# Storing new matrix-memory states from GpSimd's queue instead of SyncE's

## The reference

```
def mlstm_chunk_step(carry, inp):
    c_prev, n_prev, m_prev = carry
    q, k, v, ig, lf = inp
    ...
    num = jnp.einsum('bhls,bhsv->bhlv', s, v) + inter[..., None] * jnp.einsum('bhld,bhdv->bhlv', q, c_prev)
    ...
    c_new = decay[..., None, None] * c_prev + jnp.einsum('bhld,bhlv->bhdv', wk, v)
    n_new = decay[..., None] * n_prev + jnp.sum(wk, axis=2)
```

## Time and profile before

| what | value |
|---|---|
| three runs | 1604.52, 1608.56 and 1610.1 us; median 1608.56 |
| the profiled execution | 1613.31 us, of which the span from the first to the last instruction is 1611.6 |
| mean granted clock of TensorE | 0.914 of full speed |
| bytes moved | 532.80 MB, 331 GB/s over the span |
| stores of new states | 32 of 1024 KB |
| the matrix memory stage | about 130 to 306 us of the span |

### The profile page before, as it was taken

How to read it: one execution, slowest core, us unless ns; L and a number is a source line. 1 busy time by engine, 2 the same in 40 slices (tenths; PEclk the granted TensorE clock), 3 DMA queues, 4 the chain that set the end, 5 groups by cost and what they waited for, 6 DMA issues and landing times.

```text
span 1611.6 us, 18493 instructions
## 1 busy us (share of the span) xinstructions
PE 1336.9 (83%) x7591; PEld 748.0 (46%) x7593; DVE 519.6 (32%) x1217; ACT 191.6 (12%) x429; POOL 34.0 (2%) x72
## 2 busy tenths in 40 slices
PE   9999999999999766775785899999996656756866
PEld 6664332477754431332332577777543323323423
DVE  5647775532032220221121233630322212211222
ACT  2143232200020000000000211200200000000001
POOL 4001000000000000000000000000000000000000
PEclk8999998999989987888888999999999889888979
DMA  7335999976619999999999964452499999999995
GB/s 211 105 105 211 392 384 390 354 261 244 278 53 421 427 428 427 428 429 428 429 428 429 404 245 157 163 212 101 179 429 428 427 428 427 428 428 429 429 428 219
DMA packets 101532, 532.80 MB, mean 331 GB/s; under 512 B 6568, under 2 KB 24168, under 8 KB 76584
## 3 DMA queue, kind: packets, MB, share of 16 engines
q1 hardware_dynamic: 98536, 527.14, 80.8%
q10 hardware_dynamic: 2312, 4.20, 0.7%
q0 software_dynamic: 624, 0.62, 0.2%
HBM read 492.45 MB, written 39.49 MB: 330 GB/s over the span
## 4 chain that ended last, share of the span: by engine, by line
PE 56%; DMA 35%; DVE 4%; issue 2%; ACT 1%; SPq 1%; POOL 0%; DVEq 0%; ACTq 0%
DMA arena<-in_moe_w_up 28%; PE bank L922 24%; PE bank L1308 11%; PE bank L1330 5%; DMA out_C_s<-arena 4%; PE bank L1288 3%; PE bank L1343 3%; DMA arena<-in_state_mlstm_C 2%; PE bank L1316 1%; SPq L414 1%; PE bank L1213 1%; PE bank L1061 1%; ACT arena L786 1%; PE bank L1222 1%; PE bank L1396 1%
## 5 line engine op out<-in xcount | busy, mean ns | idle before, releaser
L1308 PE MATMUL bank<-arena,hT 128*32 128x512 f32 x2048 | 270.6, 688 | 191.4 <-DMA arena<-in_moe_w_up 178.4
L922 PE MATMUL bank<-hT,arena 128*128 128x288 f32 x1024 | 264.4, 417 | 3.3 <-issue 2.0
L1308 PEld LDWEIGHTS bank<-arena,hT 128*32 128x32 f32 x2048 | 75.0, 125 | 373.8 <-issue 373.4
L922 PEld LDWEIGHTS bank<-hT,arena 128*128 128x128 f32 x1024 | 195.7, 194 | 63.2 <-issue 5.6
L1850 DVE TENSOR_TENSOR arena<-arena,bank 64x512 f32<-64x512 f32 x32 | 22.1, 692 | 533.9 <-ACT arena L786 533.9
L1288 PE MATMUL bank<-arena 128*128 128x128 f32 (+1 forms) x864 | 157.8, 313 | 1.2 <-DVE arena L1825 0.9
L1330 PE MATMUL bank<-arena 128*32 128x512 f32 x1024 | 129.8, 651 | 21.2 <-DVE arena L1854 21.2
L1288 PEld LDWEIGHTS bank<-arena 128*128 128x128 f32 (+1 forms) x864 | 120.2, 192 | 49.6 <-issue 16.4
L922 PE MATMUL bank<-arena 128*128 128x288 f32 x512 | 127.9, 409 | 0.0
L922 PEld LDWEIGHTS bank<-arena 128*128 128x128 f32 x512 | 96.1, 190 | 30.8 <-issue 3.5
L786 ACT ACTIVATE arena<-bank 64x512 f32<-64x512 f32 x32 | 18.9, 589 | 759.6 <-PE bank L1308 759.6
(11 more groups left out here) (353 smaller groups left out, 980.6 us busy)
## 6 DMA issues: line engine op xcount, KB each, us to landing
arena<-in_moe_w_gate SPq DMA_DIRECT2D x64, 2048.0 KB, 28.4
arena<-in_moe_w_up SPq DMA_DIRECT2D x64, 2048.0 KB, 32.1
arena<-in_moe_w_down SPq DMA_DIRECT2D x64, 2048.0 KB, 25.2
arena<-in_state_mlstm_C SPq DMA_DIRECT2D x32, 1024.0 KB, 8.6
out_C_s<-arena SPq DMA_DIRECT2D x32, 1024.0 KB, 11.0
arena<-in_cmlp_w_in SPq DMA_DIRECT2D x8, 2048.0 KB, 17.5
arena<-in_mlstm_w_up SPq DMA_DIRECT2D x7, 2048.0 KB, 9.9
arena<-in_mlstm_w_down SPq DMA_DIRECT2D x4, 2048.0 KB, 18.1
```

The costliest lines, as they stand in the source:

```text
L922: ins = mm(B[m % 4][:, 0:NT], w[:, k, 128 * i:128 * i + 128], rhs(k), start=(k == 0), stop=(k == kt - 1))
L1308: ins = mm(B[j][CAP * i:CAP * i + CAP, :], xq[h][:, k, CAP * e:CAP * e + CAP], w[i][:, k, :], start=(k == 0), stop=(k == KD - 1), skip_gro ...
```

## The change

SyncE's loop keeps the waits for the stores, the loads of the states and the loads of the z pages; the waits for new states and the stores themselves go to GpSimd. There the loop over heads is written anew: the masks of head 0 come first; then, for each head, eight times a wait for a new state and its store, then the masks of the next head, then the store and the load of the normalisers as before. The semaphores are the same.

```
--- before.py
+++ after.py
@@ -361,18 +361,12 @@
             for q in range(6):
                 sp.wait_ge(s("xm_mm"), 4 * (q // 2 + 2))
                 load_state(q)
-            for q in range(NB * H + 1):
-                if q < NB * H:
-                    sp.wait_ge(s("c_new"), MH * (q + 1))
-                    sp.dma_start(state(O["C_s"], q), cview(q)).then_inc(s(f"c_stored{q % 2}"), 16)
-                if q > 0:
-
-                    r = q - 1
-                    sp.wait_ge(s(f"c_stored{r % 2}"), 16 * (r // 2 + 1))
-                    if r + 6 < NB * H:
-                        load_state(r + 6)
-                    elif r % 2 == 1:
-                        load_z((r - 27) // 2)
+            for r in range(NB * H):
+                sp.wait_ge(s(f"c_stored{r % 2}"), 16 * (r // 2 + 1))
+                if r + 6 < NB * H:
+                    load_state(r + 6)
+                elif r % 2 == 1:
+                    load_z((r - 27) // 2)
 
             sp.wait_ge(s("nums_mm"), H)
             sp.wait_ge(s("cv_stored"), 128)
@@ -515,7 +509,7 @@
                            allow_slow_non_contiguous=True).then_inc(s("m_stored"), 16)
             pool.dma_start(O["m_s"][0].rearrange("b h -> h b"), rows[32:36, NPROMPT + 3:NT:SB],
                            allow_slow_non_contiguous=True).then_inc(s("m_stored"), 16)
-            for h in range(H):
+            def masks_of_weights(h):
 
                 pool.wait_ge(s("e_ready"), 3 * (h + 1))
                 keep(ew[:, 0:128], [[1, P]], 0, -1).then_inc(s("e_masked"), 1)
@@ -523,6 +517,14 @@
                 es = ew[0:NS, 384:416].rearrange("p (b t) -> p b t", t=SB)
                 link(keep(es, [[SB, NB], [1, SB]], 0, -1))
                 keep(es, [[-SB, NB], [0, SB]], 0, 1).then_inc(s("e_masked"), 1)
+
+            masks_of_weights(0)
+            for h in range(H):
+                for q in range(NB * h, NB * h + NB):
+                    pool.wait_ge(s("c_new"), MH * (q + 1))
+                    pool.dma_start(state(O["C_s"], q), cview(q)).then_inc(s(f"c_stored{q % 2}"), 16)
+                if h + 1 < H:
+                    masks_of_weights(h + 1)
                 pool.wait_ge(s("ns_out"), h + 1)
                 pool.dma_start(n_out[h], nrow[:, h % 2, :]).then_inc(s(f"n_stored{h % 2}"), 16)
                 if h + 2 < H:
```

## The result

The changed kernel takes 1705.11 us (median of 4 runs, 1701.61 to 1707.15), the kernel before 1606.54 us beside it (4 runs, 1600.71 to 1610.1): a ratio of 1.0618, 95% interval 1.0587 to 1.0648. The forecast was 1605.3 us within 1597 to 1619. The time lies 86 us above the top of that range; the loss of 98.6 us has the sign that was given 0.25. One run further on is left out of median and ratio: experiment 1 had a tenth run of 1870.95 us at a mean granted clock of 0.674, where its nine others had 0.914 to 0.917.

A forecast was written before the change was run, and what follows sets the result against it. It took DMA transfers, almost saturated from 148 to 294 us, as the stage's bound. Start -0.3, saturated part -3.0, end 0 and GpSimd's queue 0 gave -3.3 us: 1608.6 to 1605.3 us, range 1597 to 1619.

The forecast's parts named there:

- the sign that was given 0.25: Whole kernel: the change makes it slower, chance 0.25, against 0.43 for the same and 0.32 for faster.
- the one on GpSimd's queue: Stores behind GpSimd's masks, small DMAs and `n_out` wait: delays to stores 8 and 16 covered by queued loads, 0 us.
- Rival C: GpSimd's stores cost more than SyncE's throughout: lower rate, slow issue or held issue; +6 to +10 us, chance 0.09.
- Masks: about as much time as before: 0: GpSimd's masks of the next head, now behind eight stores but ahead of the `n_out` wait: 0 us.
- rival D: VectorE's bursts of four updates hold up GpSimd's store issues, three times 2.7 us: +8 us, chance 0.03.
- Rival B: GpSimd gates the ends of heads 0 and 1, store 8 waiting until `n_out` lands: +6 us, chance 0.13.
- The gain at the start: From 142 to 148 us, loads 7 and 8 no longer stand behind stores of states not yet new: -1.7 us.
- The saturated part: From 148 to 294 us, half the distance from 392 to 409 GB/s is gained: -3.0 us (range 0 to -6.1).
- Rival A: SyncE's queue order is the limit, not the engines: about 7 us faster, 1601.6 us, chance 0.32.
- the 9.7 us: TensorE's waits for landing states, 7.7 us, plus 2.0 us ahead of the first z matmul: the cap on direct gain.

The follow-up runs named there:

- experiment 1: The changed kernel with the room for GpSimd's DMAs doubled to 2048 bytes and six store semaphores instead of two: 1610.29 us, ratio 1.0037 to the kernel before.
- experiment 2: The changed kernel with six store semaphores instead of two, the room left at 1024 bytes: 1701.27 us (one run).
- experiment 3: The changed kernel with each store as 128 rows of 8 KB instead of 512 of 2 KB, room 1024, six semaphores: 1610.7 us (one run).
- experiment 4: The changed kernel with each store as two DMAs of 256 rows, room 1024, six semaphores: 1672.15 us (one run).
- experiment 5: The changed kernel with the next head's masks made ahead of a head's last two stores, room 1024: 1700.79 us (one run).
- experiment 9: The kernel before, all on SyncE's queue, each load waiting for the store two states back instead of one: 1600.99 us, ratio 0.9988.
- Experiment 8: The changed kernel with double room and six semaphores, GpSimd holding stores 28 to 31 until z's first page landed: 1607.58 us, ratio 1.0023.

## Why the prediction was wrong

**The step that failed** is the one on GpSimd's queue, with the price of a store there. The prediction costed a store from GpSimd by its issue: "I take 1.2 us". The issue was even cheaper, 0.76 us. What the sum lacks is a term for how many stores GpSimd's queue can have under way. The largest DMA of GpSimd in the trace of before had 32 rows; 512 rows, twice, is a demand that no row there covered. Experiments 1 to 4 show that the limit is the room for this queue's DMAs: twice the room or a quarter of the rows takes the waits away, stores in halves go out three at a time and shorten the cycle to 8.06 us, and the semaphores change nothing.

**The mechanism stood in a clause, with a wrong price.** Rival C ends "if GpSimd held an issue until the store before was through", and that is what happened. It was given +6 to +10 us for the whole rival, a figure for a lower rate or a slow issue, and 0.09. Rows 6 had the bounds for it. One store at a time costs a state the time from issue to landing: 4.6 us at the shortest, 11.0 at the median. A state had about 5.4 us (2.1 MB at 392 GB/s), and 26 loads wait for a store. That is 26 x (4.6 - 5.4), so nothing, up to 26 x (11.0 - 5.4) = +146 us. The measured 8.8 gives 26 x 3.4 = +88; TensorE's last state came 87.0 us later (381.41 against 294.37). The rest, up to 95.3, is z's first page, which goes where states 26 and 27 lay and so waited for a store too: it left at 388.99 us, and the z matmuls began 12.9 us after it instead of 9.6. Such a range would have reached far past 1619. The argument given against rival C (both ways of costing an issue end by 3.1 us) spoke of the issue and not of this clause.

**"Masks: about as much time as before: 0"** was wrong as a reading (VectorE waited up to 25.1 us for them) and cost nothing by itself (experiment 5), since the states were late anyhow. Without the held stores the masks come in time: 2.8 us of waiting in experiment 1.

**What held.** Store 0 left at 135.18 us, 136.53 in experiment 1, against 136.84 worked out. The load of state 6 left at 142.21 us in experiment 1 (142.6). VectorE did not hold GpSimd's issues (0.75 to 0.81 us in experiment 1, none longer): rival D did not occur. Rival B's wait for `out_n_s` is there (8.12 us in experiment 1, ahead of store 8), but store 8 left at 178.04 us: it was held for 2.4 us after its state was new, where SyncE had held it for 2.0.

**The gain at the start** did not come, even where the stores run freely. From 142 to 148 us experiment 1 moves 288 GB/s, over 130 to 148 us 167 where the kernel before moved 174, and the load of state 8 leaves at 155.33 us, where the prediction asked for less than 152. It stood behind the landing of store 2, issued at 143.85. So the -1.7 us of the sum were wrong as well, which is little beside the 95.

**The saturated part**, tested where the stores run freely: 401 GB/s in experiment 1 and 405 in experiment 9, as the forecast said (395 to 402) and a little over. The rate came, the -3.0 us did not in experiment 1: its time is +0.1 to +0.6%. In experiment 9, where GpSimd has no part in the stores, it is -0.3% to 0, so 3 us can't be told from nothing there. The step from a higher rate to an earlier end took for granted that each single load lands no later; a median load landed 5.2 and 4.1 us later. Rival A's 7 us lie outside the interval of experiment 9 (-4.5 to +0.6 us); that the order of SyncE's queue cost a smaller part of the 9.7 us is not excluded. The Trainium skill (DMA: Bandwidth & Descriptors, section Issuing engines are not separate DMA queues) expects nothing but issue time from spreading DMAs; experiment 1, where no store is held, agrees with it (1.0037).

**Still open** in part: the 7 us between experiment 1 and the kernel before. In the profiles the z matmuls begin 6.4 us later (312.93 against 306.57). TensorE works on the last state 4.3 us later than before, behind 5.07 us of idleness. The matmuls from there to z then take 4.1 us more, those at their start at the lower clock (1.93 us for eight that took 1.07), and the 2.0 us wait ahead of z is gone. TensorE also waits for states at 194.88 and 208.16 us (1.89 and 2.83 us). Experiment 8 points to the last stores for the 5.07 us; which transfers crowd the other loads stays open. No run has a room between 1024 and 2048.

## What to carry to other kernels

Before a stream of large DMAs moves to another engine's queue, ask how many of them that queue can have under way and not only what an issue costs: count the rows of one DMA, and compare them with the largest that the queue carries in the trace. If none of that size is there, price the case of one at a time as a cycle (issue to landing, then what it releases) times the transfers on the path, however unlikely it looks. And a wait with no cause in the profile that ends each time about when the engine's own last transfer lands can be such a limit; a run with twice the room tells.

## What the runs showed of the hardware beyond that

- The same store travels in other packets from GpSimd than from SyncE. The change took 98536 - 81640 = 16896 packets from SyncE's queue (the page of before has 98536), 528 for each store, and gave GpSimd's 9328 - 624 = 8704, 272 for each: about 4 KB instead of 2 KB a packet.
- Near saturation loads landed later whichever queue the stores came from: in 13.8 us with them on GpSimd's queue and in 12.7 with all of it on SyncE's (experiments 1 and 9), against 8.6 before. An estimate of what was under way, from the median landings of a store and a load over the time of 2.1 MB at the measured rate, is 4.5 and 4.7 transfers of a state, against 3.7 before.
- TensorE's granted clock fell where it idled: in the changed kernel it is 0.55 from 180 to 200 us, where TensorE is busy for 2.57 of 20 us, so mostly at the lower of its two levels (1.2 of 2.4 GHz). The mean clock is 0.77 from 148 to 294 us, where it was 0.95, which goes with the 19.3 us more of busy time for the same matmuls.
- The Trainium skill (DMA: Bandwidth & Descriptors, section SWDGE vs HWDGE vs iDMA) says that GpSimd builds the descriptors of its DMAs itself and appends them to rings in a part of SBUF set aside for them. Experiments 1, 3 and 4 agree with it in so far as the size of a room, taken against the rows of the DMA, decides. That this room is that part of SBUF, and how many bytes a row takes there, no run here shows.
